# Feed-forward input projections: each weight fill multiplied in two halves of 256 tokens instead of 512 tokens at once

## What is computed

```python
# first block
u2 = _layer_norm(h) * (1.0 + sc2) + sh2
a, bb = jnp.split(u2 @ w_ffn_in[l], 2, axis=-1)      # 1024 -> 2 * 2816
ffn = (jax.nn.silu(a) * bb) @ w_ffn_out[l]           # 2816 -> 1024
# each of the two hybrid layers: the same shapes, with an RMS norm,
# w_ffn_gate and w_ffn_up (1024 -> 2816 each) and w_ffn_down (2816 -> 1024)
```

## Time and profile before

| | us |
|---|---|
| median of 2 runs | 3344.01 (3343.43 to 3344.58) |
| the profiled execution: its time | 3340.71 |
| the profiled execution: its span from the first to the last instruction | 3338.9 |

### The profile page before, as it was taken

One profiled execution on the slowest core, in us unless ns is written; L12 is line 12 of the kernel. 1 busy time (PEld: TensorE's weight loads), 2 busy tenths in 40 slices (PEclk: granted clock), 3 DMA queues, 4 the chain that ended last, 5 costly groups with the idle time before them and its releaser, 6 DMA issues.

```text
span 3338.9 us, 52457 instructions
## 1 busy us (share of the span) xinstructions
PE 3125.7 (94%) x20668; PEld 2497.1 (75%) x20668; DVE 1061.0 (32%) x1518; ACT 1086.8 (33%) x1515; POOL 1402.9 (42%) x1824
## 2 busy tenths in 40 slices
PE   6998989979999699999989899989999998889999
PEld 4887778848878486887667788768688766668877
DVE  5026442342110335232555311122533155431111
ACT  3355453323222334113443222222411244422222
POOL 3542244624555253222325455555322242445555
PEclk8999889989999799999999999999999999999999
DMA  4233332312333132214314233333221331423333
GB/s 191 94 93 122 109 114 82 95 50 82 94 94 103 61 120 92 71 59 146 108 61 157 77 98 96 98 104 111 84 80 63 126 132 52 154 82 95 98 96 120
DMA packets 100395, 330.78 MB, mean 99 GB/s; under 512 B 9745, under 2 KB 10001, under 8 KB 99089
## 3 DMA queue, kind: packets, MB, share of 16 engines
q1 hardware_dynamic: 73648, 273.85, 25.8%
q10 hardware_dynamic: 26592, 54.66, 4.5%
HBM read 299.64 MB, written 28.84 MB: 98 GB/s over the span
## 4 chain that ended last, share of the span: by engine, by line
issue 42%; POOL 29%; PE 24%; DVE 2%; DMA 1%; ACT 1%; DVEq 0%; POOLq 0%; SPq 0%; ACTq 0%
POOL w_lo L306 29%; PE psum L335 18%; PE psum L596 4%; DMA H<-scratch 1%; DVEq L1348 0%; PE psum L397 0%; DMA H<-in_x 0%; PE psum L402 0%; POOLq L302 0%; PE psum L792 0%; PE psum L810 0%; POOLq L312 0%; PE psum L812 0%; PE psum L772 0%; DVE arena L1645 0%
## 5 line engine op out<-in xcount | busy, mean ns | idle before, releaser
L306 POOL TENSOR_TENSOR w_lo<-w_raw,w_hi 128x256 fp32r<-128x256 f32 x1820 | 1402.7, 801 | 1927.9 <-ACT w_hi L848 1728.0
L335 PE MATMUL psum<-XH,w_hi 128*128 128x512 f32 x2720 | 1110.0, 408 | 59.6 <-DVE XL L1351 59.2
L335 PE MATMUL psum<-XH,w_lo 128*128 128x512 f32 x2720 | 1072.2, 394 | 0.0
L335 PE MATMUL psum<-XL,w_hi 128*128 128x512 f32 x2720 | 1070.8, 394 | 0.0
L335 PEld LDWEIGHTS psum<-XH,w_hi 128*128 128x128 f32 x2720 | 518.4, 191 | 202.1 <-issue 88.2
L848 ACT ACTIVATE w_hi<-w_raw 128x1024 fp32r<-128x1024 f32 x436 | 459.5, 1054 | 567.4 <-PE psum L335 521.5
L335 PEld LDWEIGHTS psum<-XL,w_hi 128*128 128x128 f32 x2720 | 517.9, 190 | 111.6
L335 PEld LDWEIGHTS psum<-XH,w_lo 128*128 128x128 f32 x2720 | 518.9, 191 | 108.8 <-issue 8.2
L335 PE MATMUL psum<-HH,w_hi 128*128 128x512 f32 x848 | 338.9, 400 | 22.9 <-DVE HL L1351 15.1
L335 PE MATMUL psum<-HL,w_hi 128*128 128x512 f32 x848 | 333.9, 394 | 0.0
L335 PE MATMUL psum<-HH,w_lo 128*128 128x512 f32 x848 | 333.9, 394 | 0.0
(11 more groups left out here) (291 smaller groups left out, 2287.8 us busy)
## 6 DMA issues: line engine op xcount, KB each, us to landing
w_raw<-in_fills SPq DMA_DIRECT2D x488, 512.0 KB, 3.5
scratch<-arena ACTq DMA_DIRECT2D x86, 256.0 KB, 2.0
arena<-scratch ACTq DMA_DIRECT2D x10, 1024.0 KB, 6.8
arena<-in_w_ada SPq DMA_DIRECT2D x4, 2048.0 KB, 20.3
H<-scratch ACTq DMA_DIRECT2D x4, 2048.0 KB, 14.8
scratch<-H SPq DMA_DIRECT2D x2, 2048.0 KB, 9.3
arena<-scratch ACTq DMA_DIRECT2D x2, 2048.0 KB, 9.6
arena<-scratch ACTq DMA_DIRECT2D x2, 1792.0 KB, 20.2
```

Source lines behind the costliest of these rows:

```text
L306: ins = nc.gpsimd.tensor_tensor(w_lo[:, to:to + FILL // 4], w_raw[:, of:of + FILL // 4], w_hi[:, to:to + FILL // 4].bitcast(F32), ALU.subt ...
L335: ins = mm(out_ap, wt[:, w:w + 128], xt[:, x0:x0 + T], start=first and k == 0 and o == 0, stop=last and k == n - 1 and o == 2)
```

## The change

The three calls of `gemm` for the feed-forward input go to a new function `gemm_halves`. It makes the 24 matmuls of a fill twice: first all of them with tokens 0 to 255 into columns 0 to 255 of bank j, then all of them with tokens 256 to 511 into columns 256 to 511. The waits before a fill, and the one signal behind its last matmul, stay where they were. The waits for the activations stand in the first half alone. Nothing else changes on any engine.

```diff
+            def gemm_halves(f, c, n, ready, skew=0):
+
+                def fill_halves(j, ready=None):
+                    for h in range(2):
+                        for k in range(8):
+                            if ready and h == 0:
+                                ready(k)
+                            w, x0 = j * FILL + k * 128, k * T + 256 * h
+                            for o, (wt, xt) in enumerate([(w_hi, XH), (w_lo, XH), (w_hi, XL)]):
+                                ins = mm(bank(j, 256, 256 * h), wt[:, w:w + 128], xt[:, x0:x0 + 256],
+                                         start=k == 0 and o == 0, stop=k == 7 and o == 2)
+                    ins.then_inc(fill_done, 1)
+
+                with pe.Fori(0, n // 4) as i:
+                    for j in range(4):
+                        pe.wait_ge(lo_ready, f + 4 * i + j + 1)
+                        pe.wait_ge(chunk_out[j], c + skew * SKEW[j] + i)
+                        fill_halves(j, None if j else ready)
...
-            gemm(88, 22, 44, ready=by_pairs("ln_x", 4))
+            gemm_halves(88, 22, 44, by_pairs("ln_x", 4))
...
-                gemm(f0 + 80, c0 + 23, 44, ready=by_pairs("rms_x", 8 * l + 4), skew=l + 1)
+                gemm_halves(f0 + 80, c0 + 23, 44, by_pairs("rms_x", 8 * l + 4), l + 1)
```

## The result

The changed kernel takes 3385.97 us (2 runs, 3385.57 to 3386.37) against 3344.01 before: ratio 1.0131, 95% interval 1.0106 to 1.0155, some 42 us slower. Timed again in turn with the kernel before, it takes 3383.79 us (4 runs) against 3344.67: ratio 1.0115, interval 1.0098 to 1.0132. The profiled execution of after has 3385.57 us and a span of 3383.8.

The account below looks back on a forecast made before the run. TensorE's matmul stride was taken to bound the three feed-forward input calls. 132 fills of 48 matmuls at 115 ns, each fill 0.080 us longer, add 10.6 us to 3344.0: 3355 us, range 3331 to 3403.

Parts of the forecast that it names:

- The likeliest case: Feed-forward input calls: excess goes with the columns, stride 115 ns, +10.6 us, 3355 us in all; chance 0.48.
- rival B: Feed-forward input matmuls: the excess is paid once for each matmul, stride 120 to 122.4 ns, 3386 to 3401 us; chance 0.32.
- The bound of the stretches: In the three feed-forward input stretches the time is TensorE's alone: number of matmuls times their stride, 226.7 ns before.
- The excess goes with the columns: 9.3 to 11.7 of the 13.3 ns over 512 columns belong to the fp32r stream; halved, 4.7 to 5.9 ns.
- the exchange: Changing from one matmul to the next, priced from float32 rows at 1.6 to 4.0 ns for each matmul.
- s = 115: Forecast stride in ns of a 256-column matmul: 106.7 of stream, 1.6 to 4.0 of exchange, 4.7 to 5.9 of excess.
- The load floor: A 128x128 weight load keeps the stride of the halves from falling under 110.7 ns, a gain of 16.7 us at best.
- Rival D: Load and stream no longer overlap wholly in the halves: stride from 124.0 ns, 3412 up to 3817 us; chance 0.09.
- Rival C: The excess vanishes in short streams and the load alone sets the stride, 110.7 ns, 3327 us; chance 0.11.
- Part 2: Load records of 188 ns outlast the 115 ns stride, but loads overlap; one at a time would cost +473 us.
- Part 3: Feeding, waits and the rest: sequencer covered, loop jump (up to +10.9 us) and starts of the calls taken as 0.

## Why the prediction was right, and which step was not

The range, 3331 to 3403, holds 3386, and the change is within 2%, as forecast. The likeliest case, 3355 with a stride of 115, is not what happened: the loss is 42 us, not 10.6, and the sign that the prediction named for its being wrong, products 11.5 us or more apart, came true. The range holds the result because it reached up to rival B, which had a chance of 0.32. That the time fell on B's lower end is in part luck: it is the sum of two costs of 6.7 ns, and not B's one of 13.3. The stride table of the runs:

| columns | load | stride, ns | over the columns, ns |
|---|---|---|---|
| 512 | fp32r, 128 wide | 226.7 | 13.3 |
| 384 | fp32r, 128 wide | 173.3 | 13.3 |
| 256 | fp32r, 128 wide | 120.0 | 13.3 |
| 192 | fp32r, 128 wide | 111.7 | load-bound |
| 128, clock 0.50 | fp32r, 128 wide | 213.3 | load-bound |
| 512 | fp32r, 64 wide | 230.0 | 16.7 |
| 256 | fp32r, 64 wide | 113.3 | 6.7 |
| 512 | bf16 every 4 bytes | 226.7 | 13.3 |
| 256 | bf16 every 4 bytes | 113.3 | 6.7 |
| 512 | bf16 packed | 215.8 | 2.5 |
| 256 | bf16 packed | 109.2 | 2.5 |

**The bound of the stretches** was read rightly: TensorE's stride alone, and nothing else moved.

**The excess goes with the columns** was right in kind. Read every 4 bytes, a stream pays 6.7 ns at 256 columns (bf16, and fp32r with half the load) and 13.3 at 512. The sum had 4.7 to 5.9 ns for it, because 1.6 to 4.0 of the 13.3 had been set aside for the exchange. In after, this part of the excess is the same per fill as before, 24 x 13.3 = 48 x 6.7, and costs nothing.

**The failed step** is the other term of s = 115: what a full fp32r load costs beside a stream nearly as short as itself. I took 1.6 to 4.0 ns from float32 rows, where a column takes two cycles (428.3 ns for 512 columns). Beside an fp32r stream of 256 columns it is 6.7 ns, which is what a load of half the width takes away (120.0 to 113.3), and 48 x 6.7 ns x 132 = 42.2 us is the whole loss. Line 529 was the nearest row, and it was still another case: its stream takes its columns at half the pace. The load floor itself (110.7 forecast, 111.7 measured at 192 columns) was right, and taking the larger of load and stream, with a little for the exchange, was not: 111.7 and 113.3 together give 120.0.

**Rival B** has the time and not the mechanism: three lengths on one line looked like a fixed 13.3 ns, until shorter loads took half of it away at 256 columns and none at 512. **Rival D** named the right place, load and stream that no longer overlap wholly, with a price of 17.3 ns over the columns where 13.3 were measured. **Rival C** did not happen. The excess didn't vanish.

**Part 2**, loads overlapping each other, was right: records of 192 ns in a stride of 120. The rule of the Trainium skill ("Perfetto Trace Analysis", section Identifying the Most-Contended Engine) that I had weighed against it pointed at the right place, but it gives no size. The loads' busy share went from 83% to 99% of the stretch (237.27 of 240 us from 755 on), and the loss did come from the loads, at a tenth of what one load at a time would cost. Yet with loads of half the width the share is 100% (100.00 of 100 us from 800 on), and there the load costs nothing: the records overlap, so a full row of them doesn't mean that the loads are at their limit.

**Part 3** was right: the sequencer, the jump of the loop and the starts of the calls show nothing. All 21 distances of the first call are 11.52 us, and the first call takes 257.96 us, of which 44 fills of 5.760 us are 253.4; before, 4.6 us were left over, now 4.5.

**Open:** why the load's share is 6.7 ns at 256 columns and nothing at 512 (at 384 it would be 3.3, if the columns' share is 10.0 there, which no run with a short load shows), and why loads of half the width cost 3.3 ns more beside 512 columns. A load of 64 columns also uses half the width of the array, so the run with it alone doesn't separate the two; the strided bf16 run, with the full width and a short load, points to the load. The 3 us by which one call in halves fell short are open too. So is what keeps the clock at 0.50 with 128 columns while it rises with 192.

## What to carry to other kernels

Keep fp32r matmuls at 512 columns where each brings a weight load of 128 columns: in halves they lost 6% of the stretch with nothing else on the critical path. Price a new length by a row with the same operand format and the same load, and when the load is nearly as long as the stream, don't take the larger of the two. Three points on a straight line are not a mechanism: vary the other partner, here the load, before believing one.

## What the runs showed beyond the expected

- With 128 columns the granted clock stayed at 0.50 through the whole call, and the kernel took 5325 us. With 192 it rose to 1.00. A cut that looks merely load-bound can lose the clock as well, and the one-column matmuls of the kernel before, whose clock fell at 37.5 us, were the row to look at.
- Operands read every 4 bytes, fp32r or bf16, stream 512 columns in 226.7 ns; packed bf16 in 215.8.
- Loading weights that are already in the array costs as much as loading new ones: the products stand 11.52 us apart either way.
